# Two middle norms taken as one, table loads and weight splits moved to earlier places, in a kernel of two transformer blocks

## The chip, the cores and the metric

One core of a Trainium2 chip. The time is that of one execution on the device in microseconds (us); the kernel before takes 3049.42, the median of 3 runs. The engines are TensorE (PE: matmuls), VectorE (DVE), ScalarE (ACT), GpSimd (POOL) and SyncE (SP, which issues most of the DMA).

## The reference, cut to what matters

There are 16 meta tokens and 512 real ones, of width 1024. The first block is attention, the HGRN2 recurrence, a gated mix of both and a mixture of 32 experts, and ends with a norm. The second block begins with its own meta tokens and another norm, and is a feed-forward part (FFN 1), a mixer of Fourier, convolution and delta branches, and a second feed-forward part (FFN 2).

```python
def rms_norm(x, w):
    y = x * lax.rsqrt(jnp.mean(x * x, axis=-1, keepdims=True) + EPS)
    return y * w
...
    # end of first_block
    h = h + moe_out.reshape(B, L, D)
    return rms_norm(h, norm_final_w)[:, N_META:]
...
    # start of second_block
    h = jnp.concatenate([meta, x], axis=1)
    h = h + 0.5 * rmsnorm(swiglu(rmsnorm(h, n[0]), ffn1_wi[l], ffn1_wo[l]), n[1])
    h = h + rmsnorm(hybrid_mixer(rmsnorm(h, n[2]), ...), n[3])
    h = h + 0.5 * rmsnorm(swiglu(rmsnorm(h, n[4]), ffn2_wi[l], ffn2_wo[l]), n[5])
```

Each expert e takes its rows of tokens and computes (silu(a) * u) @ w_out[e], where a and u are the halves of x @ w_in[e].

## The kernel before

The hidden state `hT` stays in SBUF with the 1024 features on 8 x 128 partitions and the 528 tokens along the free dimension. Everything runs through in one program. Each engine has its own instruction order, which follows the order of the Python code, and semaphores tie the orders together.

**Split products.** A product in float32 is taken as three products of fp32r parts: each weight tile of 128x1024 is cast on ACT (`cast_act`, L424), and the rest, weight minus cast, is formed on DVE (`rest_dve`, L430). The input `uT` is cast on ACT (`high_act`, L459) into `fuh` or another `...uh`, and its rest formed on DVE (`low_dve`, L465). `Split` holds the weight tiles of a stage; SP loads them some tiles ahead into the slots of `ring`. Every stage begins by casting the first two or three tiles.

**Norm.** For each of 8 feature tiles ACT squares (`square_act`, L335), PE adds over the partitions by a product with a matrix of ones (`sum_pe`), ACT takes Ln (L374) and Exp with the factor -0.5 (L377), and DVE scales (`scale_dve`, L384). Ln and Exp stand in different tables of ACT. An activation of one element on `warm` (L371) loads the table of Ln ahead of it.

**Joins.** Between attention, `Hgrn`, `MixOut`, the experts and what follows, all engines but SP wait for the last signals of the stage in front (`join`, L269). At the start of `Hgrn` DVE also zeroes `Kl` and `sc` (L1088, L1089), and makes the rests of the three tiles of head 0. Attention goes in 32 steps of a head and a block of queries: PE scores, DVE `sm` (the row maximum, L717), ACT exp into `P` (L658), DVE reciprocal and scale, PE transpose, PE product.

**Route and Experts.** `Route` sends each token to two experts; `gates` is the weight of each row, `ov` the number of blocks beyond the 64 rows that an expert has (0 here). Weights come in chunks of 1 MB, 4 for w_in and 2 for w_out of each expert, issued on SP as slots come free. For expert e PE computes in(e) (4 chunks, from `exT`), then turns the product of e-1 (`turn_pe`, L1733) and computes out(e-1) (2 chunks, from `ehT`). Two experts' outputs are put into one tile `uT`, split into `uTr`, and put on their tokens by products with a matrix of zeros and ones, `eto` (`to_pe`): 8 for each pair of experts, 4 in each expert's turn, one behind each chunk of in(e). DVE adds each to `hT` (`add_dve`, L1806). `pool` gathers rows of tokens from DRAM.

**Overflow and BlockEnd.** After the last expert each engine reads `ov` (`values_load`, L1843) and branches around the code for further blocks (L1861), which ends in a barrier of all engines. `BlockEnd` takes the final norm of the first block in place on `hT` (with the weights `fin`), loads the second block's meta tokens, `m2T`, into the first 16 columns, and squares and sums again for the first norm of FFN 1, whose root and scaling stand in `Ffn`. `ConvFourier.act`, the first stage of the mixer, issues 7 DMA of Fourier tables from ACT's queue (L2343, L2344).

## Time and profile before

| | us |
|---|---|
| median of 3 runs (lowest, highest) | 3049.42 (3048.24, 3050.43) |
| the profiled execution: its time, its span | 3054.2, 3052.9 |
| PE busy in the span | 2751.3 (90%) |
| DVE, ACT, GpSimd busy | 1218.6, 933.0, 153.2 |
| mean granted clock of TensorE | 0.955 of full speed |

The span is the time in the records of one profiled execution. Busy shares are means over stages that have different limits. In the windows below the columns are the busy time of each engine, in brackets its number of instructions, then PEclk, the granted clock of TensorE as a share of 2.4 GHz (0.50 is the level of 1.2 GHz), the mean busy share of the 16 DMA engines, and what they moved.

### The profile page before, as it was taken

To read this page: it belongs to the slowest core of one execution; us is meant where nothing else is said; L and a number is where in the kernel's file an instruction comes from. 1 tells how busy PE (TensorE), PEld (TensorE's weight loads), DVE (VectorE), ACT (ScalarE), POOL (GpSimd) and SP (SyncE) were. 2 spreads that over 40 slices of the span, in tenths; PEclk is the share of its full clock that TensorE was granted. 3 is DMA by queue.
4 is the path that set the end of the run, shared out by engine and by line. 5 is a ranking of instruction groups with operands and counts; after the bars stand their busy time and mean duration, and the time that the engine had idled before them with its cause. 6 is when DMAs were issued, how large, how long until landed. Compare 5 with 4: busy or idle time off the path is not lost. (4 is left out here: it accounts for less than half of the span.)

```text
span 3052.9 us, 38074 instructions
## 1 busy us (share of the span) xinstructions
PE 2751.3 (90%) x15996; PEld 2092.7 (69%) x15996; DVE 1218.6 (40%) x2176; ACT 933.0 (31%) x1354; POOL 153.2 (5%) x210
## 2 busy tenths in 40 slices
PE   7989999898789988879999879898989898799997
PEld 6768888675333333359999878687868775578785
DVE  4346666534333333343333433243534334533334
ACT  4235555323111111142121341343434322422222
POOL 0000000000100000000000000121212110000000
PEclk9999999998899999989999989998989999899998
DMA  3012111234999999722222122111111122222221
GB/s 128 15 63 66 59 59 53 76 105 175 347 392 396 390 396 397 322 77 89 92 84 87 59 93 70 65 46 45 51 40 53 38 66 94 76 95 89 92 90 56
DMA packets 79177, 388.21 MB, mean 127 GB/s; under 512 B 9224, under 2 KB 9608, under 8 KB 53792
## 3 DMA queue, kind: packets, MB, share of 16 engines
q1 hardware_dynamic: 71856, 357.14, 32.5%
q0 software_dynamic: 5424, 23.35, 2.2%
q10 hardware_dynamic: 1728, 5.28, 0.5%
q8 instruction: 129, 2.11, 0.3%
q14 instruction: 40, 0.33, 0.0%
HBM read 375.10 MB, written 10.62 MB: 126 GB/s over the span
## 5 line engine op out<-in xcount | busy, mean ns | idle before, releaser
L197 PE MATMUL ps<-uTr,ringr 128*128 128x512 f32 (+1 forms) x1408 | 416.3, 342 | 0.0
L197 PE MATMUL ps<-muh,ringr 128*128 128x264 f32 (+1 forms) x1504 | 381.5, 346 | 25.2 <-DVE uTr L465 17.2
L197 PE MATMUL ps<-buh,ringr 128*128 128x512 f32 (+1 forms) x1312 | 352.7, 356 | 21.0 <-DVE ringr L430 15.5
L430 DVE TENSOR_TENSOR ringr<-ring,ringr 128x1024 fp32r<-128x1024 f32 (+1 forms) x215 | 257.6, 1210 | 255.2 <-ACT ringr L424 254.9
L197 PE MATMUL ps<-fuh,ringr 128*128 128x264 f32 (+1 forms) x1296 | 282.9, 324 | 19.2 <-DVE ful L465 19.2
L197 PEld LDWEIGHTS ps<-muh,ringr 128*128 128x128 f32 x1504 | 250.1, 196 | 53.1 <-issue 23.3
L424 ACT CAST ringr<-ring 128x1024 fp32r<-128x1024 f32 (+1 forms) x215 | 219.2, 1037 | 163.2 <-DMA ring<-in_w_fi 37.9
L197 PEld LDWEIGHTS ps<-uTr,ringr 128*128 128x128 f32 x1408 | 248.4, 195 | 24.4 <-issue 3.1
L197 PEld LDWEIGHTS ps<-buh,ringr 128*128 128x128 f32 x1312 | 222.4, 192 | 54.1 <-issue 26.1
L197 PEld LDWEIGHTS ps<-fuh,ringr 128*128 128x128 f32 x1296 | 203.3, 190 | 42.5 <-issue 18.6
L197 PE MATMUL ps<-rmore,exT 128*64 128x512 f32 x736 | 180.0, 612 | 7.7 <-DMA rmore<-in_w_ein 5.8
L197 PE MATMUL ps<-ful,ringr 128*128 128x264 f32 (+1 forms) x648 | 174.4, 324 | 0.0
L1806 DVE TENSOR_TENSOR hT<-hT,ps 128x512 f32<-128x512 f32 x128 | 87.7, 687 | 207.1 <-PE ps L197 207.0
L2122 DVE TENSOR_TENSOR fsg<-ps,fsg 128x528 f32<-128x528 f32 (+1 forms) x44 | 30.8, 699 | 301.7 <-PE ps L197 301.7
L197 PE MATMUL ps<-fhh,ringr 128*128 128x264 f32 (+1 forms) x576 | 126.3, 326 | 4.4 <-DVE fhl L465 4.4
L197 PEld LDWEIGHTS ps<-eto,uTr 128*128 128x128 f32 x256 | 39.1, 192 | 126.2 <-issue 122.0
L1767 ACT COPY exT<-ps 128x512 f32<-128x512 f32 x32 | 18.7, 585 | 339.1 <-PE ps L201 339.1
L197 PEld LDWEIGHTS ps<-rmore,exT 128*64 128x64 f32 x736 | 50.4, 138 | 99.2 <-issue 84.9
L197 PE MATMUL ps<-eto,uTr 128*128 128x512 f32 x256 | 93.7, 452 | 25.3 <-DVE uTr L1796 24.8
L197 PEld LDWEIGHTS ps<-ful,ringr 128*128 128x128 f32 x648 | 109.2, 190 | 9.6
L459 ACT CAST fhh<-fsg 128x528 fp32r<-128x528 f32 (+1 forms) x44 | 27.6, 627 | 254.0 <-DVE fsg L2122 254.0
L197 PE MATMUL ps<-rmore,ehT 128*64 128x512 f32 x384 | 87.7, 597 | 17.5 <-DVE ehT L1780 16.4
(436 smaller groups left out, 4473.7 us busy)
## 6 DMA issues: line engine op xcount, KB each, us to landing
rmore<-in_w_ein SPq DMA_DIRECT2D x92, 1024.0 KB, 27.6
rmore<-in_w_eout SPq DMA_DIRECT2D x48, 1024.0 KB, 27.7
ring<-in_w_ein SPq DMA_DIRECT2D x36, 1024.0 KB, 28.8
ring<-in_w_fi SPq DMA_DIRECT2D x54, 512.0 KB, 3.7
fmore<-in_w_fi SPq DMA_DIRECT2D x34, 512.0 KB, 3.8
ring<-in_w_hg SPq DMA_DIRECT2D x32, 512.0 KB, 3.8
ring<-in_w_eout SPq DMA_DIRECT2D x16, 1024.0 KB, 28.9
ring<-in_w_out SPq DMA_DIRECT2D x32, 512.0 KB, 3.8
```

What stands on the lines that cost most here:

```text
L197: return self.P.matmul(out, lhsT, rhs, start=start, stop=stop, skip_group_check=True)
L424: self.k.A.copy(self.halves(i)[0], self.part(i)).then_inc(self.cast.next(), 1)
L430: self.k.V.tensor_tensor(low, self.part(i), high.bitcast(F32), SUB).then_inc(self.rest.next(), 1)
L459: (self.k.A.copy(h, src) if scale == 1.0 else self.k.A.mul(h, src, scale)).then_inc(self.high.next(), 1)
L1767: A.copy(self.xT[:, e % 2].rearrange("p a c -> p (a c)"), k.ps[:, self.bank("x", e), :]).then_inc(self.x_out.next(), 1)
L1806: k.V.tensor_tensor(h, h, k.ps[:, self.bank("to", n), :], ADD).then_inc(self.added.next(), 1)
L2122: V.tensor_tensor(self.row(s), self.acc(self.bank[i + 1]), self.row(s), MUL).then_inc(self.prod.next(), 1)
```

## The change

1. `Norm.table_act`: the load of Ln's table goes ahead of the first square, instead of behind the last. That holds for every norm.
2. At three joins the first tiles' casts and rests are made in the stage in front: of head 0's tiles in attention's steps 25 to 30 (the loads too), of `MixOut`'s first two in `Hgrn`'s last steps, and in `Ffn` and `ConvFourier` all but the first tile are cast and their rests made between the scalings of the norm. `Kl` and `sc` are zeroed on GpSimd, behind the issue of the spill of `hT`.
3. `m2T` is loaded at the start of `Route.pool`; its 16 columns' norm is taken in small pieces (`meta_dve`, `meta_pe`, `meta_act`) at the first expert.
4. All five engines wait for `ov` and read it ahead of the experts. The barrier of all engines behind the branch goes.
5. In the experts the four products with `eto` of an expert's turn stand behind chunks 1 to 3 and behind `turn_pe`, instead of behind chunks 0 to 3. DVE's adds follow: three at the start of a turn and the fourth behind the product with the gates.
6. `BlockEnd` becomes one norm of the 512 real columns. Its 8 squares are summed twice: on PE with the weights fin² + EPS in the columns' place of the ones (bank 6), and on DVE into `acc`, which one product with ones then sums over the partitions (bank 7). Two Ln and one Exp give the scale of the first norm of block 2 at once; `uT` is `hT` times that times `fin` times the gain. The scaling of `hT` itself comes later: an Exp behind `Ffn`'s casts (`late_act`) and 8 DVE instructions in the second group of FFN 1 (`late_dve`). Before, there were 8 scalings of `hT`, a second set of 8 squares, 16 sums of 264 columns and a second Ln.
7. The 7 DMA of Fourier tables go from ACT's queue to GpSimd's.

```diff
+    def table_act(self):
+        self.k.A.activation(self.k.warm, self.k.eps, ACT.Ln)
     def square_act(self, x, m, *values):
         k = self.k
+        if m == 0:
+            self.table_act()
...
-        k.A.activation(k.warm, k.eps, ACT.Ln)
...
+                if n in (25, 27, 29):
+                    self.ahead.cast_act((n - 25) // 2)
...
+                if n in (26, 28, 30):
+                    self.ahead.rest_dve((n - 26) // 2)
...
+    def pool(self):
+        G = self.k.G
+        G.memset(self.Kl, 0.0).then_inc(self.zero.next(), 1)
+        G.memset(self.sc, 0.0).then_inc(self.zero.next(), 1)
...
+                if h == 9 and n in (4, 5):
+                    self.ahead.cast_act(n - 4)
...
-        V.memset(self.Kl, 0.0).then_inc(self.zero.next(), 1)
-        V.memset(self.sc, 0.0).then_inc(self.zero.next(), 1)
...
+                    self.ahead.rest_dve(n - 4)
...
-        W.cast_act(0)
-        W.cast_act(1)
...
-        W.rest_dve(0)
-        W.rest_dve(1)
...
+        G.dma_start(k.hT[:, :, 0:NM], k.a["m2T"]).then_inc(k.ld_m2.landing(), 16)
...
+        self.nxt.meta_dve()
...
+                if e == 0:
+                    self.nxt.meta_pe()
             else:
-                for n in self.steps(e):
+                for n in self.steps(e)[0:3]:
                     self.to_pe(n)
             if e + 1 < NE:
                 self.rows_pe(e + 1)
             if e:
                 self.turn_pe(e - 1)
+                for n in self.steps(e)[3:]:
+                    self.to_pe(n)
...
-            if beside:
-                self.to_pe(beside[c])
+            if beside and c:
+                self.to_pe(beside[c - 1])
...
+            for n in self.steps(e)[0:3]:
...
+            for n in self.steps(e)[3:]:
+                self.add_dve(n)
+            if e == NE:
+                self.nxt.weights_dve(self.comb.at(4 * NE - 8))
...
-        nc.all_engine_barrier()
...
+    def meta_dve(self):
+        k, V, x = self.k, self.k.V, self.k.hT[:, :, 0:NM]
+        y = k.sq[:, 0, 0:8 * NM].rearrange("p (a c) -> p a c", a=8)
+        V.wait_ge(*k.ld_m2.at(16))
+        V.tensor_tensor(y, x, x, MUL).then_inc(self.small.next(), 1)
...
+        self.table_act()
         for m in range(8):
-            self.norm.square_act(k.hT, m)
-        self.norm.root_act()
+            if m >= 2:
+                k.A.wait_ge(*self.sumsq.at(m - 1))
+                k.A.wait_ge(*self.gathered.at(m - 1))
+            k.A.activation(k.sq[:, m % 2, 0:S], k.hT[:, m, NM:L], ACT.Square).then_inc(self.square.next(), 1)
...
+        k.take(6, 7)
+        P.wait_ge(*self.weighted.at(1))
         for m in range(8):
-            self.nxt.square_act(k.hT, m, self.norm.scaled.at(m + 1), k.ld_m2.at(16))
-    def pe(self):
+            P.wait_ge(*self.square.at(m + 1))
+            k.mm(k.ps[:, 6, :], self.weights[:, 128 * m:128 * m + 128], k.sq[:, m % 2, 0:S], m == 0, m == 7).then_inc(
+                self.sumsq.next(), 1)
+        P.wait_ge(*self.gathered.at(8))
+        k.mm(k.ps[:, 7, :], k.ones, self.acc, True, True).then_inc(self.mean.next(), 1)
...
+    def root_act(self):
+        k, rb, r = self.k, self.k.rb[:, NM:L], self.k.sq[:, 0, 0:S]
+        k.A.wait_ge(*self.sumsq.at(8))
+        k.A.activation(rb, k.ps[:, 6, :], ACT.Ln, bias=k.eps2[:, 0:1], scale=1.0 / D).then_inc(self.log.next(), 1)
+        k.A.wait_ge(*self.mean.at(1))
+        k.A.activation(r, k.ps[:, 7, :], ACT.Ln, bias=k.eps[:, 0:1], scale=1.0 / D).then_inc(self.rlog.next(), 1)
+        k.A.wait_ge(*self.log.at(1))
+        k.A.activation(rb, rb, ACT.Exp, scale=-0.5).then_inc(self.root.next(), 1)
...
+            V.wait_ge(*self.root.at(1))
+        V.scalar_tensor_tensor(out=out[:, m, c], in0=x[:, m, c], scalar=k.fin[:, 1, m:m + 1], in1=k.rb[:, c], op0=MUL,
+                               op1=MUL).then_inc(self.scaled.next(), 1)
...
             exp.sp()
+            exp.first_pool()
+            for eng in (k.P, k.V, k.A, k.G, k.SP):
+                eng.wait_ge(*route.blocks.last())
+            count = k.nc.values_load(route.ov[0:1, 0:1], min_val=0, max_val=NOV - 1)
...
-        for i in range(3):
-            W.cast_act(i)
+        W.cast_act(0)
         self.norm.root_act()
         for m in range(8):
             self.norm.high_act(self.pu, m)
+            if m in (3, 6):
+                W.cast_act(m // 3)
...
+            if m in (5, 7):
+                W.rest_dve(m // 2 - 1)
...
+                if g == 1:
+                    self.norm.late_dve(j)
...
-        for n in range(NC2):
-            A.dma_start(self.dft[:, n].rearrange("p a c -> p (a c)"), k.a["dft"][n]).then_inc(self.there[n].landing(), 16)
-        A.dma_start(self.dfs, k.a["dfs"]).then_inc(self.there_s.landing(), 16)
...
+        G.dma_start(self.dfs, k.a["dfs"]).then_inc(self.there_s.landing(), 16)
+        for n in range(NC2):
+            G.dma_start(self.dft[:, n].rearrange("p a c -> p (a c)"), k.a["dft"][n]).then_inc(self.there[n].landing(), 16)
```

Line numbers in the rows of the changed kernel below are its own: L430 of before is L443, L717 is L736, L335 is L342, L1733 is L1768, L197 is L198 and L1806 is L1847.

PE in the turn of expert 31 and behind it, before (`exT` is the input of in(e), `ehT` of out(e), `eto,uTr` the products with the matrix of zeros and ones, `con,eact` is `turn_pe`; a row "x2" is one `to_pe`):

```order
L197 MATMUL ps<-rmore,exT 64x512 x4
L197 MATMUL ps<-eto,uTr 128x512 x2
L1733 MATMUL ps<-con,eact 128x64 x4
L197 MATMUL ps<-rmore,ehT 64x512 x8
L197 MATMUL ps<-eto,uTr 128x512 x8
L1733 MATMUL ps<-con,eact 128x64 x4
L197 MATMUL ps<-rmore,ehT 64x512 x8
L197 MATMUL ps<-eto,uTr 128x512 x16
L1843 TENSOR_LOAD ov
```

The same place in the changed kernel:

```order
L198 MATMUL ps<-rmore,exT 64x512 x4
L198 MATMUL ps<-eto,uTr 128x512 x2
L1768 MATMUL ps<-con,eact 128x64 x4
L198 MATMUL ps<-eto,uTr 128x512 x2
L198 MATMUL ps<-rmore,ehT 64x512 x8
L198 MATMUL ps<-eto,uTr 128x512 x6
L1768 MATMUL ps<-con,eact 128x64 x4
L198 MATMUL ps<-eto,uTr 128x512 x2
L198 MATMUL ps<-rmore,ehT 64x512 x8
L198 MATMUL ps<-eto,uTr 128x512 x16
L211 COMPARE_AND_BRANCH
```

One product with `eto` now stands between `turn_pe` and the product that waits for DVE's copy of what was turned, and the read of `ov` is gone from here.

ACT from the end of the experts to FFN 1's first casts, before:

```order
L1861 UNCONDITIONAL_BRANCH
L335 ACTIVATE sq<-hT 128x512 x8
L371 ACT_TABLE_LOAD
L371 ACTIVATE warm<-eps 128x1
L374 ACTIVATE rb<-ps,eps 128x512
L377 ACT_TABLE_LOAD
L377 ACTIVATE rb<-rb 128x512
L335 ACTIVATE sq<-hT 128x528 x8
L424 CAST ringr<-ring 128x1024 x3
L371 ACT_TABLE_LOAD
L371 ACTIVATE warm<-eps 128x1
L374 ACTIVATE rb<-ps,eps 128x528
```

In the changed kernel (`fuh` is the high part of `uT`):

```order
L333 ACT_TABLE_LOAD
L333 ACTIVATE warm<-eps 128x1
L2040 ACTIVATE sq<-hT 128x512 x8
L437 CAST ringr<-ring 128x1024
L2078 ACTIVATE rb<-ps,eps 128x512
L2080 ACTIVATE sq<-ps,eps 128x512
L2082 ACT_TABLE_LOAD
L2082 ACTIVATE rb<-rb 128x512
L472 CAST fuh<-uT 128x528 x4
L437 CAST ringr<-ring 128x1024
L472 CAST fuh<-uT 128x528 x3
L437 CAST ringr<-ring 128x1024
```

Eight squares, three table loads and two casts of weights no longer stand ahead of the first cast of `uT`; one further Ln does.

DVE at the end of attention and the start of `Hgrn`, before (`sm` is the maximum of a row of scores, `P` the exp of them, `PT` its transpose, `lbv` and the like are small constants of `Hgrn`):

```order
L722 TENSOR_SCALAR P<-P,sm 128x528
L728 COPY PT<-ps 128x384
L728 COPY PT<-ps 128x512
L1075 TENSOR_TENSOR lbv<-vec 128x8
...
L1087 TENSOR_SCALAR hnh<-vec 128x1
L1088 MEMSET hKl 128x3584
L1089 MEMSET hsc 128x1024
L430 TENSOR_TENSOR ringr<-ring,ringr 128x1024 x3
L1110 TENSOR_SCALAR hfs<-hfs,omv,lbv 128x528
```

In the changed kernel, from the copy ahead of step 30 (steps 26 and 28 have such a row as well):

```order
L747 COPY PT<-ps 128x128
L443 TENSOR_TENSOR ringr<-ring,ringr 128x1024
L736 TENSOR_REDUCE sm<-ps 128x1
L739 RECIPROCAL sm<-sm 128x1
L741 TENSOR_SCALAR P<-P,sm 128x400
L747 COPY PT<-ps 128x256
...
L1118 TENSOR_SCALAR hnh<-vec 128x1
L1141 TENSOR_SCALAR hfs<-hfs,omv,lbv 128x528
L1146 TENSOR_SCALAR hk<-hfs 128x528
```

A rest of a weight tile now stands ahead of a row maximum in attention, and the two memsets and three rests are gone from the start of `Hgrn`.

## Rows read from the trace of the kernel before

**Rows 1.** The page, busy time, share of the span and instructions of each engine:

```profile
PE 2751.3 (90%) x15996; PEld 2092.7 (69%) x15996; DVE 1218.6 (40%) x2176; ACT 933.0 (31%) x1354; POOL 153.2 (5%) x210
```

**Rows 2.** Timeline, first norm: start, us, engine, line, operation, [idle before <-releaser]

```profile
18.48 1.28 ACT L371 ACT_TABLE_LOAD   x1
```

**Rows 3.** DVE's waits, attention's last steps (172 to 197 us): total, times, longest

```profile
DVE sm L717 <- PE ps L197: 2.9, 4, 0.8
```

**Rows 4.** Timeline, start of `Hgrn`

```profile
196.36 0.58 ACT L668 COPY oaT<-ps 128x512 f32<-128x512 f32 x1 [2.28 <-PE ps L197]
...
199.50 3.04 DVE L1088 MEMSET hKl<- 128x3584 f32 x1 [0.69 <-issue]
...
203.53 3.43 DVE L430 TENSOR_TENSOR ringr<-ring,ringr 128x1024 fp32r<-128x1024 f32 x3
...
204.95 0.78 PE L197 MATMUL ps<-buh,ringr 128*128 128x264 f32 x2 [8.62 <-DVE ringr L430]
```

**Rows 5.** Window behind that start (columns as told above)

```profile
205.00:211.00 6.00, 6.00 (x27) 6.00 (x28) 1.96 (x2) 0.00 (x0) 0.00 (x0) 0.50 0.00 0
```

**Rows 6.** Timeline, from `Hgrn` to `MixOut`

```profile
587.87 2.94 ACT L424 CAST ringr<-ring 128x1024 fp32r<-128x1024 f32 x3 [1.55 <-DVE oh L1204]
...
590.52 0.77 PE L197 MATMUL ps<-buh,ringr 128*128 128x512 f32 x1 [6.87 <-DVE ringr L430]
```

**Rows 7.** Timeline, end of `Route` and first expert

```profile
781.69 1.11 PE L201 MATMUL ps<-con,xg 64*128 64x64 f32 x8
...
783.24 0.58 ACT L1767 COPY exT<-ps 128x512 f32<-128x512 f32 x1 [23.09 <-PE ps L201]
...
783.92 4.78 PE L197 MATMUL ps<-rmore,exT 128*64 128x512 f32 x12 [1.12 <-DVE rgates L1608]
...
784.77 0.13 DVE L1615 CAST ov<-rnb 1x1 int32<-1x1 f32 x1
787.63 0.33 SPq L250 DMA_DIRECT2D rmore<-in_w_eout  x1
```

**Rows 8.** A window in the experts

```profile
800.00:1030.00 230.00, 209.28 (x1006) 76.95 (x1004) 77.21 (x113) 33.59 (x52) 13.91 (x15) 1.00 1.01 390
```

**Rows 9.** PE's waits in the experts (790 to 1300 us): total, times, longest

```profile
PE ps L197 <- DVE uTr L1796: 24.8, 16, 3.2
PE ps L197 <- DVE ehT L1780: 22.1, 30, 0.9
```

**Rows 10.** Timeline, end of the experts

```profile
1247.79 8.65 SPq L250 DMA_DIRECT2D rmore<-in_w_eout  x4
...
1289.16 3.65 PE L197 MATMUL ps<-rmore,ehT 128*64 128x512 f32 x16 [0.93 <-DVE ehT L1780]
...
1295.98 6.59 PE L197 MATMUL ps<-eto,uTr 128*128 128x512 f32 x16 [3.17 <-DVE uTr L1796]
```

**Rows 11.** The page's DMA issues: operation, count, KB each, median us from issue to landing

```profile
rmore<-in_w_eout SPq DMA_DIRECT2D x48, 1024.0 KB, 27.7
```

**Rows 12.** Timeline, `BlockEnd` to FFN 1

```profile
1307.81 0.63 ACT L335 ACTIVATE sq<-hT 128x512 f32<-128x512 f32 x1 [13.19 <-PEq L1861]
...
1318.68 0.67 ACT L374 ACTIVATE rb<-ps,eps 128x512 f32<-128x512 f32 x1
...
1337.36 0.64 ACT L377 ACTIVATE rb<-rb 128x528 f32<-128x528 f32 x1
...
1340.42 0.78 PE L197 MATMUL ps<-fuh,ringr 128*128 128x264 f32 x2 [8.10 <-DVE ful L465]
```

**Rows 13.** Timeline, FFN 1 to the mixer

```profile
1758.74 2.85 ACTq L2343 DMA_DIRECT2D dft<-in_dft  x6
...
1770.53 0.78 PE L197 MATMUL ps<-muh,ringr 128*128 128x264 f32 x2 [11.88 <-DVE uTr L465]
```

**Rows 14.** Timeline, the mixer to FFN 2

```profile
2642.72 2.94 ACT L424 CAST ringr<-ring 128x1024 fp32r<-128x1024 f32 x3 [1.26 <-PE ps L197]
```

**Rows 15.** GpSimd's groups by form: busy, mean ns, idle before

```profile
L3194 POOL TENSOR_TENSOR nDT<-nDT,nKK 88x528 f32<-88x528 f32 x8 | 12.5, 1561 | 17.1 <-DVE nMT L3107 17.1
```

More of the change, by code:

```diff
@@ L1335, in block1 @@
             k.G.dma_start(k.spill1, k.hT).then_inc(k.spilled.landing(), 16)
+            rec.pool()
             rec.sp()
+            for w, n in (("w_oh", 8), ("w_o", 4)):
+                for m in range(n):
+                    for x in range(2):
+                        W2.load(k.a[w][m, :, 1024 * x:1024 * x + 1024])
             rec.pe()
@@ L1340, in block1 @@
             k.join(*rec.sigs, k.spilled)
-            k.sig.close(loads)
+            k.sig.close(loads + W2.sigs)
         norm = Norm(k, NM, True)
-        mix = MixOut(k, st, oh, branch.gt, norm)
-        mix.sp()
+        mix = MixOut(k, st, oh, branch.gt, norm, W2)
         mix.pe()
@@ L1937, in dve, with __init__, constants_dve, meta_pe @@
         ins.then_inc(self.summed.next(), 1)
-class BlockEnd:
-    def __init__(self, k, nxt):
-        self.k, self.norm, self.nxt = k, Norm(k, NM), nxt
-        k.ld_m2 = k.sig.pdma("m2")
-    def pool(self):
-        k = self.k
-        k.G.dma_start(k.hT[:, :, 0:NM], k.a["m2T"]).then_inc(k.ld_m2.landing(), 16)
+class BlockEnd(Norm):
+    def __init__(self, k):
+        Norm.__init__(self, k, 0)
+        sig = k.sig
+        flat = k.uT.rearrange("p a c -> p (a c)")
+        self.weights, self.acc = flat[:, 0:1024], flat[:, 2048:2560]
+        k.ld_m2 = sig.pdma("m2")
+        self.small, self.weighted, self.gathered, self.scale_h = (sig.dve(n) for n in (
+            "fsmall", "fweights", "fgathered", "fscaled"))
+        self.msum, self.mlog, self.mroot = sig.pe("msum"), sig.act("mlog"), sig.act("mroot")
+        self.mean, self.rlog, self.rroot = sig.pe("fmean"), sig.act("rlog"), sig.act("rroot")
+        self.sigs += [self.small, self.weighted, self.gathered, self.scale_h, self.msum, self.mlog, self.mroot, self.mean,
+                      self.rlog, self.rroot, k.ld_m2]
+    def constants_dve(self):
+        k, V, g, fin = self.k, self.k.V, self.k.vec["fin"], self.k.fin
+        V.memset(k.eps2, EPS * EPS).then_inc(self.small.next(), 1)
+        V.tensor_tensor(fin[:, 0, :], g, g, MUL).then_inc(self.small.next(), 1)
+        V.tensor_tensor(fin[:, 1, :], g, k.vec["g"][:, 0:8], MUL).then_inc(self.small.next(), 1)
+        V.wait_ge(*self.small.at(2))
+        V.tensor_scalar(fin[:, 0, :], fin[:, 0, :], EPS, None, ADD).then_inc(self.small.next(), 1)
+    def meta_dve(self):
[3 more added lines that the diff above has]
+        V.tensor_tensor(y, x, x, MUL).then_inc(self.small.next(), 1)
+    def meta_pe(self):
+        k = self.k
+        k.take(7)
+        k.P.wait_ge(*self.small.at(5))
+        for m in range(8):
+            ins = k.mm(k.ps[:, 7, 0:NM], k.ones, k.sq[:, 0, NM * m:NM * m + NM], m == 0, m == 7)
+        ins.then_inc(self.msum.next(), 1)
+        k.give((7,), self.mlog.at(1))
+    def meta_act(self):
+        k, A, rb = self.k, self.k.A, self.k.rb[:, 0:NM]
+        A.wait_ge(*self.msum.at(1))
+        A.activation(rb, k.ps[:, 7, 0:NM], ACT.Ln, bias=k.eps[:, 0:1], scale=1.0 / D).then_inc(self.mlog.next(), 1)
+        A.wait_ge(*self.mlog.at(1))
+        A.activation(rb, rb, ACT.Exp, scale=-0.5).then_inc(self.mroot.next(), 1)
@@ L1960, in pe, with weights_dve, dve @@
+    def weights_dve(self, free):
+        k, V = self.k, self.k.V
+        V.wait_ge(*free)
         for m in range(8):
-            self.norm.sum_pe(m)
+            ins = V.tensor_scalar(self.weights[:, 128 * m:128 * m + 128], k.ones, k.fin[:, 0, m:m + 1], None, MUL)
+        ins.then_inc(self.weighted.next(), 1)
+    def dve(self):
+        k, V = self.k, self.k.V
         for m in range(8):
-            self.nxt.sum_pe(m)
-    def dve(self):
-        k = self.k
-        for m in range(8):
-            self.norm.scale_dve(k.hT, [k.vec["fin"][:, i:i + 1] for i in range(8)], k.hT, m)
+            V.wait_ge(*self.square.at(m + 1))
+            if m:
+                V.wait_ge(*self.gathered.at(m))
+                V.tensor_tensor(self.acc, self.acc, k.sq[:, m % 2, 0:S], ADD).then_inc(self.gathered.next(), 1)
+            else:
+                V.tensor_copy(self.acc, k.sq[:, 0, 0:S]).then_inc(self.gathered.next(), 1)
@@ L1971, in experts, with late_act, late_dve @@
+    def late_act(self):
+        k, r = self.k, self.k.sq[:, 0, 0:S]
+        k.A.wait_ge(*self.rlog.at(1))
+        k.A.activation(r, r, ACT.Exp, scale=-0.5).then_inc(self.rroot.next(), 1)
+    def late_dve(self, m):
+        k, h = self.k, self.k.hT[:, m, NM:L]
+        k.V.wait_ge(*self.rroot.at(1))
+        k.V.scalar_tensor_tensor(out=h, in0=h, scalar=k.vec["fin"][:, m:m + 1], in1=k.sq[:, 0, 0:S], op0=MUL,
+                                 op1=MUL).then_inc(self.scale_h.next(), 1)
 def experts(k, norm, free, kept):
+    end = BlockEnd(k)
@@ L1974, in experts @@
     with ExitStack() as st:
-        route = Route(k, st, norm)
+        route = Route(k, st, norm, end)
+        end.constants_dve()
         route.pe()
@@ L1987, in experts @@
             exp.pool()
-            k.join(*exp.sigs, *exp.got, route.blocks)
+            k.join(*exp.sigs, *exp.got)
             k.SP.wait_ge(*exp.added.last())
-            k.SP.wait_ge(*route.blocks.last())
         with ExitStack() as st2:
-            Overflow(k, st2, route).run()
-    nxt = Norm(k, 0)
-    end = BlockEnd(k, nxt)
+            Overflow(k, st2, route).run(count)
     end.pe()
```

118 lines of the change are left out of this document (72 added, 46 removed).

## The prediction

> **What bounds the kernel now.** I read the page first: PE is busy for 2751.3 us of 3052.9 [rows 1]. So the time that is left to win lies in the stretches where PE waits. The list of waits by line then says what PE waits for. The timeline of each stretch says which chain of instructions ends last. Last, windows by stage tell whether PE or the DMA sets the pace. Two kinds of stretch appear. At the joins of stages PE stands still for 8.62 us before `Hgrn` [rows 4], 6.87 before `MixOut` [rows 6], 8.10 before FFN 1 behind two norms in a row [rows 12] and 11.88 before the mixer [rows 13]. There a chain on ACT and DVE bounds the time. In the experts PE waits in many small pieces for DVE [rows 9], but the 16 DMA engines are busy without a gap, share 1.01 [rows 8]. The sum goes from the start of the program to its end.
>
> **First norm.** Ln's table load, 1.28 us [rows 2], goes ahead of the squares, where ACT waits for its input. ACT has casts to make until right before it, so all of it is on the path: gain 1.3.
>
> **Attention to Hgrn.** PE can start when the last copy of attention ends, at 196.36 + 0.58 = 196.9, and starts at 204.95 [rows 4]. The three rests and two memsets are all that is between, so the gain is up to 8.0; I take 7.9. Right behind the start six us run at a granted clock of 0.50, with 27 matmuls [rows 5]; at full clock they would take 3.0. The engine had stood still for 8.6 us before. With no such stop I expect most of it back, 2.6, between 0 and 3.0. Against it, attention is lengthened. Three rests of 1.22 (3.43 for three that overlap a little, rows 4) come ahead of the row maxima of steps 26, 28 and 30. In eight steps DVE waits four times for the scores, 2.9 in all, 0.8 at the longest [rows 3]; the three rests meet about three of these waits, 2.3 us. So 3.7 - 2.3 = 1.4 are lost, and 3.7 at most. Sum: 7.9 + 2.6 - 1.4 = 9.1.
>
> The memsets go behind a DMA issue on GpSimd. The nearest row there is a tensor-tensor of 528 elements in 1.56 us [rows 15], which for 3584 and 1024 elements would make 10.6 and 3.0. DVE takes 3.04 and 0.91 [rows 4], the lower bound. Even 13.6 from 198 ends at 212, and `Kl` is first written some 30 us behind the start of `Hgrn`. Cost 0.
>
> The Trainium skill (SBUF — State Buffer, Who interferes with whom) speaks against this: a `tensor_scalar` of DVE can take a pair of ports that it shares with GpSimd, and whichever engine issues first holds them for the whole instruction. By that rule the two `TENSOR_SCALAR` of DVE that make `hfs` and `hk` would stand until the memset is done. No row of before has such a pair at once; by the rule the sum would be up to 2 us worse, and without it it takes 0.
>
> **Hgrn to MixOut.** PE starts at 590.52, the first cast at 587.87 [rows 6]. With both made earlier 2.65 go. One rest of 1.2 now stands ahead of the last copy that the chain needs, and the cast ahead of it waits for a gate; half is hidden at a guess, bounds 0 and 1.2. Gain 1.9.
>
> **Route.** This one loses. The first expert's product starts at 783.92, while DVE is at work on `ov` until 784.77 + 0.13 = 784.90 [rows 7]. Now every engine waits for `ov` and reads it before its first expert instruction. The small square of `meta_dve` adds 0.3, the read 0.5 (no row shows it; bounds 0 and the 4.5 that read, branch and barrier take together below), then come the eight transposes of the first rows, 1.1, the copy of 0.58 [rows 7] and 0.4 of handing over: 787.7. DMA goes on only when PE frees a slot, at 787.63 today [rows 7], so all of it shifts too. Loss 3.8, bounds 3 and 7.
>
> **Experts.** PE goes from 783.92 [rows 7] to the start of out(31) at 1289.16 [rows 10] in 32 turns of 15.8 us. The waits for `uTr`, 24.8, and `ehT`, 22.1 [rows 9], are 1.5 of each; work is 14.3. Moving one product with `eto` behind `turn_pe` (0.8 = 6.59 / 8, rows 10) covers the waits of 0.7 for `ehT`, and starting them one chunk later, 1.9 or more, covers most of those of 1.5 for `uTr`. Is that 47 us? The 14 slots are filled before the experts, and the other 178 of 192 chunks land between 787.63 and the last landing. The last of four issues, 8.65 in all, begins at 1254.3 [rows 10], and 27.7 later [rows 11] is 1282.0. That makes 2.78 per chunk and 16.7 per expert, at a DMA share of 1.01. So DMA sets the body's pace now, and PE only lives off the lead of 14 chunks. A faster PE will use up that lead and wait for chunks: body 0.
>
> At the end it counts. Out(31) ends at 1289.16 + 3.65 = 1292.8 [rows 10], 10.8 behind the last landing. PE that keeps up is through with out(30) at 1278.8: its last chunk lands two chunks of 2.5 (1 MB at 420 GB/s, an estimate for the end of the stream) before 1282.0, and half of 3.65 follows. Then come three products with `eto` 2.5, a turn 0.5, one more 0.8, and out(31) 3.65; with 0.5 for handing over it ends at 1286.8. Gain 6.0, bounds 3 and 7.
>
> **Overflow, BlockEnd, FFN 1.** The experts' last add ends 0.7 behind the products, 1295.98 + 6.59 + 0.7 = 1303.3 = T [rows 10]. PE starts FFN 1 at 1340.42 = T + 37.1 [rows 12]. After the change: branch, table load and its activation 1.6 (the load now stands behind the branch, where nothing hides it); squares and sums 1318.68 - 1307.81 = 10.9 as today; one product with ones 1.0; Ln 0.67, table 1.28; and from the start of Exp to PE's start 1340.42 - 1337.36 = 3.1 [rows 12, 2]. That is 18.5, a gain of 18.6. The barrier, the 8 scalings, the second squares, sums and Ln are gone with it. DVE's sums of squares, 0.7 each, run beside PE's of 1 us. Against it, two rests of 1.22 are now inside the chain of scalings and rests which feeds PE until its end: 2.4. Gain 16.2. At full clock the sums would be 2.9 shorter.
>
> **FFN 1 to the mixer.** From 1758.74 the Fourier issues hold ACT for 3.4, the second cast 1.0, and table and activation 1.4, all ahead of Ln [rows 13, 14]; one rest inside the chain costs 1.2. Gain 4.6. The tables on GpSimd's queue are first wanted some 30 us later: cost 0.
>
> **Mixer to FFN 2.** Two casts of the three in 2.94 [rows 14] and table and activation: 3.4, less two rests: 0.9.
>
> **Nothing.** `meta_pe`, `meta_act` with three table loads and `weights_dve` stand in the experts, where DVE and ACT are idle for two thirds and more [rows 8]; `late_act` and the 8 `late_dve` in FFN 1, where PE bounds. Without that cover they would be some 2, 5, 1 and 6 us.
>
> **Sum.** 1.3 + 9.1 + 1.9 - 3.8 + 0 + 6.0 + 16.2 + 4.6 + 0.9 = 36.2. The profiled execution took 3054.2, 4.8 over the median of the runs. 3054.2 - 36.2 = 3018.0, and as a median 3013.
>
> **Rivals.** *Less is won (0.17).* The clock stays at half speed behind each join (-2.6), the rests cost attention all of 3.7 (-2.3), the experts start 7 us late (-3.2), the tail gives 3 (-3), the rest before `MixOut` is all on the path (-0.6): 12 less, 3025. For it speaks that the window behind the join is slow today; against it, that these are several small things.
>
> *More is won (0.14).* The sums run at full clock (2.9) and the rests at the joins hide (2.4, 1.2, 2.4): 9 more, 3004. The 6 us stop before the squares is gone, which speaks for it; that DVE has no gap in these chains, against it.
>
> *The memset is in the way (0.08).* GpSimd's memset lasts to 212 by the bound above. `hfs` comes on DVE some 9 us behind PE's start, at about 206; if DVE has to stand until 212, the rest of the next tile behind it is done at 214, about when PE comes to it: 0 to 2 us, 3015. The skill's sentence on the shared ports is for it, GpSimd's unknown pace (3 to 10.6 us) leaves it open.
>
> *The body is PE's (0.03).* If DMA can go faster when it is asked sooner, the 47 us less the 6 already counted come on top: 2972. The share of 1.01 speaks against it.
>
> *Slower (0.04).* PE's waits turn into waits for chunks. If the granted clock, 1.00 today [rows 8], falls to half for a share s of the experts, PE's work is 14.3 x (1 + s). It passes DMA's 16.7 at s = 0.17, and eats the 36 us at s = 0.25, since each 0.01 is 4.6 us. At a third of the time it is 3054. PE's busy share doesn't fall against today's, which speaks against it.
>
> **How the numbers follow.** The forecast itself has 0.54, 3013 with 3008 to 3020 as its own range. To leave out no more than two in ten I reach over the case of more and that of less, with some us beyond for the bound of 7 at the experts' start and of 0 for the clock: 3002 to 3029. A change under 0.2% (6 us) can't be told from none here. Faster 0.94, the same 0.02, slower 0.04.
>
> **What would show it.** In the changed profile: PE's start of `Hgrn` near 198 and `MixOut` without a stop; the first expert's product about 3 us behind the last cast of `ov`; waits for `uTr` and `ehT` replaced by waits for `rmore`; out(31) within 5 us of the last landing; 18 to 21 us from the last add to FFN 1. Wrong would be: a granted clock of 0.5 in the experts, a DMA share clearly below 1, or attention longer by over 4 us.

## The result and the profile after

The changed kernel takes 3014.97 us, the median of 4 runs (3012.9 to 3016.04), beside 3049.93 for the kernel before on the same chip (3048.24 to 3053.38). The ratio is 0.9883, with an interval of 0.9866 to 0.99. The forecast was 3013 with a range of 3002 to 3029. Of the kernel before there are two profiled executions in all, of 3052.9 and 3046.9 us span, and of the changed one three, of 3014.7, 3007.4 and 3016.0. The first of each is read here, the others where it matters.

The page of the changed kernel: PE is as busy as before and the span shorter, so the time came out of PE's stops.

```profile
span 3014.7 us, 38051 instructions
PE 2750.9 (91%) x15982; PEld 2090.1 (69%) x15982; DVE 1224.6 (41%) x2197; ACT 927.6 (31%) x1347; POOL 161.5 (5%) x219
```

**Start of `Hgrn`.** Timeline of the changed kernel, the columns as in [rows 4]:

```profile
194.44 0.59 ACT L685 COPY oaT<-ps 128x512 f32<-128x512 f32 x1 [2.28 <-PE ps L198]
195.13 0.48 PE L198 MATMUL ps<-buh,ringr 128*128 128x264 f32 x2 [0.72 <-PE ps L198]
196.15 3.11 POOL L910 MEMSET hKl<- 128x3584 f32 x1
196.66 3.53 DVE L1117 TENSOR_SCALAR omv<-lbv 128x8 f32<-128x8 f32 x1
199.18 0.97 POOL L911 MEMSET hsc<- 128x1024 f32 x1
201.92 0.56 DVE L1141 TENSOR_SCALAR hfs<-hfs,omv,lbv 128x528 f32<-128x528 f32 x1 [1.73 <-ACT hfs L1043]
```

PE's stop of 8.62 [rows 4] is 0.72. GpSimd zeroes `hKl` in 3.11, hardly slower than DVE's 3.04, and nothing like the bound of 10.6. The row to look at is DVE's: a `TENSOR_SCALAR` of 8 elements takes 3.53 us, and ends at 200.19, when GpSimd's second memset ends (199.18 + 0.97). The next large DVE instruction, `hfs`, begins at 201.92, behind its own input.

The window behind the start:

```profile
197.00:203.00 6.00, 6.00 (x44) 5.63 (x43) 4.23 (x5) 2.00 (x4) 3.16 (x2) 1.00 0.85 339
```

The granted clock is 1.00 where it was 0.50 [rows 5], 44 matmuls in 6 us for 27.

**Hgrn to `MixOut`.** Timeline:

```profile
566.11 1.98 ACT L437 CAST ringr<-ring 128x1024 fp32r<-128x1024 f32 x2
567.17 1.23 DVE L443 TENSOR_TENSOR ringr<-ring,ringr 128x1024 fp32r<-128x1024 f32 x1 [1.91 <-ACT ringr L437]
568.32 0.68 DVE L1228 COPY ho<-ps 128x512 f32<-128x512 f32 x1
575.17 0.80 PE L198 MATMUL ps<-buh,ringr 128*128 128x512 f32 x1 [4.27 <-DVE oh L1235]
```

PE starts 0.05 behind `oh` instead of 2.68 [rows 6]. The copy of `ho` stands behind the rest and begins 1.4 behind its product instead of 0.04. From its start to the end of `oh` it is 0.8 shorter, so the rest costs 0.6.

**Route and the first expert.** Timeline:

```profile
765.68 0.14 DVE L1644 CAST ov<-rnb 1x1 int32<-1x1 f32 x1
766.64 1.08 PE L202 MATMUL ps<-con,xg 64*128 64x64 f32 x8 [4.27 <-DVE ov L1644]
768.45 8.76 PE L198 MATMUL ps<-rmore,exT 128*64 128x512 f32 x32 [0.72 <-issue]
772.09 2.04 SPq L251 DMA_DIRECT2D rmore<-in_w_eout  x2
```

The transposes of the first rows now wait 4.27 for `ov`. The product starts 2.6 behind the end of the cast of `ov`; before it began 1.0 ahead of that [rows 7]. SP goes on 3.6 behind the product, as before.

**The experts.** PE's waits from 770 to 1285 us, total, times, longest:

```profile
PE ps L198 <- DMA rmore<-in_w_ein: 20.2, 16, 2.3
PE ps L198 <- DMA ring<-in_w_ein: 10.6, 8, 2.3
```

And a window, with the columns of [rows 8]:

```profile
1000.00:1200.00 200.00, 179.50 (x820) 63.86 (x818) 65.86 (x97) 27.55 (x43) 10.85 (x12) 0.97 1.01 396
```

PE no longer waits for `uTr` and `ehT` [rows 9] but for chunks of the weights, 31 us in all for 47 before. The DMA share is 1.01, as before [rows 8]. The granted clock is 0.97 in this window: short patches at the lower clock appear. Up to the start of out(31) there are six, of 3.4 us each, where the experts had one before.

**End of the experts, FFN 1.** Timeline:

```profile
1230.76 8.67 SPq L251 DMA_DIRECT2D rmore<-in_w_eout  x4
1267.00 3.65 PE L198 MATMUL ps<-rmore,ehT 128*64 128x512 f32 x16 [0.26 <-DVE ehT L1817]
1280.09 1.28 DVE L1847 TENSOR_TENSOR hT<-hT,ps 128x512 f32<-128x512 f32 x2 [0.23 <-PE ps L198]
1281.57 1.28 ACT L333 ACT_TABLE_LOAD   x1 [9.10 <-DVE hT L1847]
1282.97 1.13 ACT L2040 ACTIVATE sq<-hT 128x512 f32<-128x512 f32 x2
1292.74 1.02 PE L198 MATMUL ps<-uT,o 128*128 128x512 f32 x2
1298.77 0.78 PE L198 MATMUL ps<-fuh,ringr 128*128 128x264 f32 x2 [5.01 <-DVE ful L478]
1306.21 0.52 PE L198 MATMUL ps<-fuh,ringr 128*128 128x264 f32 x2 [1.06 <-DVE ful L478]
```

The last of four issues of weights begins at 1237.3, and out(31) starts 29.7 later, where it was 34.9 [rows 10]. Against the landing of the last chunk it starts 0.6 behind and ends 4.3 behind; before, these were 7.2 and 10.8. From the first product to that landing it is 497.9 us, and it was 498.1. PE starts FFN 1 17.4 behind the last add (1280.09 + 1.28). In the last row it waits for a low part that stands behind a rest.

**Mixer and FFN 2.** Timeline:

```profile
1719.99 3.18 POOL L2490 DMA_DIRECT2D dft<-in_dft  x6
1724.89 0.78 PE L198 MATMUL ps<-muh,ringr 128*128 128x264 f32 x2 [6.03 <-DVE uTr L478]
2612.24 0.77 PE L198 MATMUL ps<-fuh,ringr 128*128 128x512 f32 x1 [5.96 <-DVE ful L478]
```

The stop before the mixer is 6.03 instead of 11.88 [rows 13]. That before FFN 2 is 5.96 and was 9.36:

```profile
2652.00 0.77 PE L197 MATMUL ps<-fuh,ringr 128*128 128x512 f32 x1 [9.36 <-DVE ful L465]
```

### The profile page after: what moved, and what is told of

It is laid out like the page before. It is cut to its first block and busy times, and to the rows that moved or that the text cites. A ratio compares the mean times of both kernels' runs of the same rounds, so it can differ in the third digit from the quotient of the medians.

```text
span 3014.7 us, 38051 instructions
## 1 busy us (share of the span) xinstructions
PE 2750.9 (91%) x15982; PEld 2090.1 (69%) x15982; DVE 1224.6 (41%) x2197; ACT 927.6 (31%) x1347; POOL 161.5 (5%) x219
## 5 line engine op out<-in xcount | busy, mean ns | idle before, releaser
L198 PE MATMUL ps<-uTr,ringr 128*128 128x512 f32 (+1 forms) x1408 | 415.8, 341 | 0.0
L198 PE MATMUL ps<-muh,ringr 128*128 128x264 f32 (+1 forms) x1504 | 384.1, 348 | 20.0 <-DVE uTr L478 11.9
L443 DVE TENSOR_TENSOR ringr<-ring,ringr 128x1024 fp32r<-128x1024 f32 (+1 forms) x215 | 258.5, 1211 | 252.7 <-ACT ringr L437 252.1
L198 PE MATMUL ps<-buh,ringr 128*128 128x512 f32 (+1 forms) x1312 | 350.3, 353 | 9.8 <-DVE oh L1235 4.3
L198 PE MATMUL ps<-fuh,ringr 128*128 128x264 f32 (+1 forms) x1296 | 283.3, 324 | 16.0 <-DVE ful L478 15.9
L198 PEld LDWEIGHTS ps<-muh,ringr 128*128 128x128 f32 x1504 | 253.1, 198 | 47.8 <-issue 17.5
L198 PEld LDWEIGHTS ps<-uTr,ringr 128*128 128x128 f32 x1408 | 247.5, 195 | 23.6 <-issue 3.1
L198 PEld LDWEIGHTS ps<-buh,ringr 128*128 128x128 f32 x1312 | 220.8, 190 | 42.8 <-issue 8.9
L198 PEld LDWEIGHTS ps<-fuh,ringr 128*128 128x128 f32 x1296 | 204.1, 191 | 39.6 <-issue 12.6
L198 PE MATMUL ps<-rmore,exT 128*64 128x512 f32 x736 | 181.5, 622 | 21.7 <-DMA rmore<-in_w_ein 20.2
L1847 DVE TENSOR_TENSOR hT<-hT,ps 128x512 f32<-128x512 f32 x128 | 87.7, 688 | 219.2 <-PE ps L198 218.2
L198 PE MATMUL ps<-ful,ringr 128*128 128x264 f32 (+1 forms) x648 | 174.8, 324 | 0.0
L198 PEld LDWEIGHTS ps<-rmore,exT 128*64 128x64 f32 x736 | 52.8, 140 | 121.7 <-issue 85.3
L198 PE MATMUL ps<-fhh,ringr 128*128 128x264 f32 (+1 forms) x576 | 124.9, 323 | 4.4 <-DVE fhl L478 4.4
L198 PEld LDWEIGHTS ps<-ful,ringr 128*128 128x128 f32 x648 | 108.8, 190 | 9.1
L198 PEld LDWEIGHTS ps<-fhh,ringr 128*128 128x128 f32 x576 | 90.0, 189 | 13.6 <-DVE fhl L478 5.0
L198 PEld LDWEIGHTS ps<-eto,uTr 128*128 128x128 f32 x256 | 39.9, 195 | 85.8 <-issue 79.8
L198 PE MATMUL ps<-eto,uTr 128*128 128x512 f32 x256 | 95.7, 459 | 4.0 <-DVE uTr L1837 3.2
```

The source lines that it names most:

```text
L198: return self.P.matmul(out, lhsT, rhs, start=start, stop=stop, skip_group_check=True)
L443: self.k.V.tensor_tensor(low, self.part(i), high.bitcast(F32), SUB).then_inc(self.rest.next(), 1)
L1847: k.V.tensor_tensor(h, h, k.ps[:, self.bank("to", n), :], ADD).then_inc(self.added.next(), 1)
```

## The experiments

All but the controls and the last undo or alter one thing in the changed kernel. A whole execution of one and the same kernel varies by several us from one to the next. So most verdicts rest on a stretch between two instructions in the profile, and the time of the whole is given beside it.

### Controls

The first profiles held a surprise: from PE's start of the mixer to its start of FFN 2 it took 881.5 us before and 887.4 after, though the stop at the end of this stretch is 3.4 shorter, and the rest at its start costs only 1.1 (see the rests below). The stretch to compare lies between: from DVE's last low part at the mixer's start to ACT's first square for FFN 2. PE's matmuls and DVE's instructions there are the same and in the same order in both kernels; the loads of Ln's table stand elsewhere in the norms, so that ACT has one more in the stretch, and the 7 DMA of Fourier tables come from another queue.

> The kernel before, profiled once more. Between the first squares of the mixer and those of FFN 2 the changed kernel took some 8 us longer than the kernel before, with the same instructions there. Theory: this is where patches of the lower granted clock fall in one execution, so this second profile of the same kernel has that stretch differ from the first by up to 4 us or more, with the low patches in other places. Rival: the change itself slows the mixer; then this stretch agrees with the first profile within 1 us.

> The changed kernel, profiled once more. Theory: the mixer's stretch comes out shorter or longer than in its first profile by several us, and the sum of low-clock time explains it at half its length. Rival: it is again 8 us longer than in the kernel before, whatever the clock does.

The kernel before took 3048.25, the changed one 3008.71. The stretch between, in the first profiles of both kernels and in that of the kernel with the tables back on ACT's queue (an experiment below):

```profile
1778.95:2631.60 852.65, 767.42 (x4911) 629.68 (x4909) 316.86 (x520) 290.80 (x419) 116.34 (x163) 0.94 0.18 59
1734.45:2595.46 861.01, 773.83 (x4911) 633.15 (x4909) 316.88 (x520) 292.15 (x422) 116.92 (x163) 0.93 0.19 58
1738.60:2591.96 853.36, 768.34 (x4911) 630.87 (x4909) 316.83 (x519) 292.12 (x421) 116.22 (x163) 0.94 0.18 59
```

The second profile of the kernel before gives 852.8, within 0.1 of its first. So the first expectation failed, and what came is what its rival had named. The changed kernel gives 861.0, 854.4 and 857.3 in its three profiles. The eight other kernels below that have the tables on GpSimd's queue lie between 854.1 and 859.0 (in two of them a rest of 1.1 moves into the stretch and is counted in it). All eleven are longer than the kernel before, by 4.2 in the mean without that rest. The mixer is slower in the changed kernel, and a part of what the joins win is lost there.

The second expectation holds in kind: the changed kernel's two profiles differ by 6.6. In the stretch the first has 120.3 us at the lower clock and the second 110.1; the 10.2 are worth 5.1 at half speed, most of the 6.6. The kernel before has 103 in both. So the loss looks like the clock's: 7 to 17 us more at the lower level. What in the change brings the patches isn't shown. The one kernel with the tables on ACT's queue has 102.8 us at the lower clock and 853.4 in all, nearly as before. That is a single profile, and it makes the queue of the tables the first suspect, no more.

### The order of products in the experts

```diff
-            if beside and c:
-                self.to_pe(beside[c - 1])
+            if beside:
+                self.to_pe(beside[c])
```

The fourth product behind `turn_pe` and the split of DVE's adds go too.

> The changed kernel with the four products with ones of an expert's turn back behind chunks 0 to 3, and the adds back at the head of the turn. Theory (DMA sets the body's pace): the last landing moves by under 1 us against the first product, PE waits for ehT and uTr again, and out(31) ends 5 to 7 us later; the kernel takes 6 us more than the changed one, ratio to before about 0.990 to 0.991. Rival (PE sets the pace): the body is some 40 us longer, ratio about 1.0.

Waits of this kernel, 770 to 1300 us:

```profile
PE ps L198 <- DVE uTr L1833: 23.5, 15, 3.2
PE ps L198 <- DVE ehT L1815: 22.4, 30, 0.9
PE ps L198 <- DMA rmore<-in_w_ein: 3.8, 3, 1.5
```

The waits of before are back, 46 us, and the time isn't. From the first product to the last add it takes 517.9 us; the changed kernel takes 512.9, 512.6 and 514.3 in its three profiles, and before it was 519.4 and 518.1. So 46 us of waits are worth 3.5 to 5.3. They count at the end: the last chunk lands 497.9 us behind the first product, as in the changed kernel's first profile, and out(31) starts 5.6 behind that landing instead of 0.6. DMA sets the pace of the body, and the rival that PE does is out by 35 us. The whole took 3017.17 (0.9889, interval 0.9872 to 0.9906), which fits and tells nothing by itself.

The order also moves the clock. Between the first product and out(31) this kernel has no patch at the lower clock behind the first 5 us, and the kernel before none or one. The changed kernel has six, six and four, and the eight others with its order three to six. DMA's pace hides them there.

### Head 0's splits

```diff
-                if n in (25, 27, 29):
-                    self.ahead.cast_act((n - 25) // 2)
...
-                if n in (26, 28, 30):
-                    self.ahead.rest_dve((n - 26) // 2)
```

`Hgrn` then makes them at its start. The memsets stay on GpSimd.

> The changed kernel with the casts and rests of head 0's first three tiles back at the start of Hgrn; the memsets stay on GpSimd. Theory 1 (the clock follows PE's stop, and GpSimd's memset holds DVE up): DVE's small tensor_scalar stand until the memset of 3.1 us ends, the first rest follows, PE starts 5.5 to 6.5 us behind the last copy of attention in place of 0.7, and the window behind it runs at 0.5 for some 6 us, which costs 2.5 more; attention is 0.7 shorter. In all 7 to 8 us more than the changed kernel. Rival A (no port is held): PE starts 3.5 behind the copy. Rival B (the clock's patch has nothing to do with the stop): the window stays at 1.0, 5 us more in all.

Timeline of its start of `Hgrn`, and the window behind:

```profile
192.66 3.10 POOL L906 MEMSET hKl<- 128x3584 f32 x1
193.17 3.51 DVE L1113 TENSOR_SCALAR omv<-lbv 128x8 f32<-128x8 f32 x1
193.46 3.22 DVE L443 TENSOR_TENSOR ringr<-ring,ringr 128x1024 fp32r<-128x1024 f32 x1
195.68 0.97 POOL L907 MEMSET hsc<- 128x1024 f32 x1
196.98 0.78 PE L198 MATMUL ps<-buh,ringr 128*128 128x264 f32 x2 [6.06 <-DVE ringr L443]
```

```profile
197.00:203.00 6.00, 6.00 (x28) 6.00 (x29) 0.00 (x0) 0.00 (x0) 0.00 (x0) 0.51 0.22 93
```

Theory 1 holds at the join. DVE's `TENSOR_SCALAR` ends at 196.68, with GpSimd's second memset (196.65). The first rest behind it ends at 196.68 too, 3.22 where one takes 1.22: PE starts 2.0 later than by its own work. PE starts 5.4 behind the copy of attention's last output (0.1 in the changed kernel), and behind the stop the clock is 0.51, where the changed kernel has 1.00. From the copy's end to `hfs` it is 14.8 us against 6.9: 7.9 lost, of which 2.6 are the clock's. Attention is 0.5 shorter: from the 25th row maximum to the last copy it takes 24.0, as in both profiles of the kernel before, and 24.5 in the changed kernel.

The whole disagrees: 3012.91 (0.9873, interval 0.9855 to 0.9891), no slower than the changed kernel. An expected 7 us should show beside an interval of some 5, and doesn't. Its profile doesn't win the time back in one place; against the second profile of the changed kernel it ends 8.3 later, against the first 1.0 later. That the stop costs over 7 us there is shown; that the kernel as a whole is 7 us slower is not.

### The memsets

```diff
-        G.memset(self.Kl, 0.0).then_inc(self.zero.next(), 1)
+        V.memset(self.Kl, 0.0).then_inc(self.zero.next(), 1)
```

The same for `sc`, at DVE's place of before, with the splits of head 0 in attention.

> The changed kernel with the two memsets of Hgrn on DVE, the splits of head 0 still in attention. Theory: DVE's small tensor_scalar are back at 0.17 us, its memsets end about 4 us later, hfs waits for PE's product anyway, and its distance from PE's start of Hgrn stays 6.8 us; the move to GpSimd of the memsets by itself buys and costs nothing. Rival 1 (the port pair cost up to 2 us): hfs comes earlier here. Rival 2: hfs comes later here, since the memsets on DVE end behind the product.

DVE's timeline of this kernel:

```profile
196.91 0.17 DVE L1115 TENSOR_SCALAR omv<-lbv 128x8 f32<-128x8 f32 x1
197.83 3.04 DVE L1117 MEMSET hKl<- 128x3584 f32 x1 [0.69 <-DVE hnh L1116]
202.17 0.56 DVE L1141 TENSOR_SCALAR hfs<-hfs,omv,lbv 128x528 f32<-128x528 f32 x1 [0.22 <-ACT hfs L1041]
```

The small instruction is back at 0.17, so its 3.5 was GpSimd's memset. `hfs` comes 6.8 behind PE's start in both kernels. The theory holds: with the splits in attention, moving the memsets is worth nothing. 3012.80 in one run.

### The barrier

```diff
+        nc.all_engine_barrier()
```

behind the branch, where it was.

> The changed kernel with the barrier of all engines behind the branch put back. Theory: it holds every engine for about 3.5 to 4 us behind the last add (the 4.5 that read, branch and barrier took before, less 0.5 for the read), so FFN 1 starts 21 to 22 us behind the last add in place of 17.5, and the sums may run at the lower clock, some us more. Rival: ACT's table load, 1.5 us, goes on beside it and the squares lose only 2 us.

```profile
1282.68 1.28 ACT L333 ACT_TABLE_LOAD   x1 [12.96 <-PEq L1903]
1300.55 0.78 PE L198 MATMUL ps<-fuh,ringr 128*128 128x264 f32 x2 [5.00 <-DVE ful L478]
```

FFN 1 starts 21.9 behind the last add, which ends at 1278.65, instead of 17.4: 4.5. The table load doesn't go on beside the barrier: it starts 4.0 behind the last add instead of 0.2, so the barrier holds it for 3.8, and GpSimd's `DRAIN` takes 3.58 of that. The other 0.7 are the 16 sums on PE, 9.8 for 9.2: in the whole stretch 10.7 us are at the lower clock, for 4.7. 3012.64 in one run.

### The Fourier tables

> The changed kernel with the 7 DMA issues of Fourier tables back on ACT's queue. Theory: ACT casts and takes Ln 3.3 to 3.4 us later, and PE stands still 9.4 us before the mixer in place of 6.0. Rival: a part of the issues hides behind PE's sums, and the stop grows by 2 us or less.

The edit puts the two loops of issues back ahead of `W.cast_act(0)`.

```profile
1719.53 3.02 ACTq L2489 DMA_DIRECT2D dft<-in_dft  x6
1729.03 0.78 PE L198 MATMUL ps<-muh,ringr 128*128 128x264 f32 x2 [9.59 <-DVE uTr L478]
```

A stop of 9.59 for 6.03: the issues were wholly on the path at this join, 3.6. 3009.62 in one run, which is no longer than the changed kernel: the mixer behind the join takes 853.4, as told under the controls, and from FFN 2's start to the end it is 399.3 for 402.5, with 20.4 us at the lower clock for 27.0. So whether the move of the tables wins anything in the whole stays open; one profile can't tell.

### Rests behind the last low part

```diff
-            if m in (5, 7):
-                W.rest_dve(m // 2 - 1)
         self.pu.low_dve(k.uT[:, 7, r0:L], k.uh[:, 7, r0:L], self.ul[:, 7, r0:L], 7)
+        W.rest_dve(1)
+        W.rest_dve(2)
```

and in the mixer's first stage the same with its one rest.

> The changed kernel with the rests of the second and third weight tile of both FFNs, and of the second of the mixer, behind the last low part of the input instead of between the scalings. Theory: PE walks through the first tile behind DVE's low parts, so a rest in that chain costs its whole 1.22; behind it, it hides under PE's last products of the first tile and the second tile's 6 us. Gain about 2 at each FFN and 1 at the mixer, 5 us against the changed kernel. Rival: PE waits for the rest of the second tile instead, and nothing or under 1 us is won at each.

DVE's timeline at FFN 1:

```profile
1305.32 0.71 DVE L478 TENSOR_TENSOR ful<-uT,fuh 128x528 fp32r<-128x528 f32 x1 [0.28 <-ACT fuh L472]
1305.95 2.35 DVE L443 TENSOR_TENSOR ringr<-ring,ringr 128x1024 fp32r<-128x1024 f32 x2
```

From PE's start to the end of the last low part it is 8.5, 8.4 and 8.4 us at FFN 1, the mixer and FFN 2, for 10.4, 9.6 and 10.3: 1.9, 1.1 and 1.9 won, 4.9 in all. PE doesn't wait for these rests. The theory holds. 3005.92 (0.9855, interval 0.9839 to 0.9872), 9 below the changed kernel's median; what is beyond 4.9 isn't explained, and whole runs vary by as much.

### The first expert ahead of the read

```diff
+            exp.head_pe()
+            exp.rows_act(0)
             for eng in (k.P, k.V, k.A, k.G, k.SP):
                 eng.wait_ge(*route.blocks.last())
```

`head_pe` holds the first rows' transposes and in(0).

> The changed kernel with the first expert's rows, their copy on ACT and its product in(0) issued on PE and ACT ahead of the wait for ov and its read. Theory: the product starts when the gates' matmuls end, as before the change, 3 to 4 us earlier against the gates' copy on DVE, all of the stream of weights shifts with it and the kernel takes 3.5 us less than the changed one. Rival: the wait moves with the read to behind in(0) and holds PE up there by as much, while DMA, which has 4 free slots by then, still gains; then 3.5 as well at the last landing, but PE waits behind in(0).

```profile
762.67 1.08 PE L202 MATMUL ps<-con,xg 64*128 64x64 f32 x8 [1.06 <-DMA xg<-vrow,idx]
764.56 4.70 PE L198 MATMUL ps<-rmore,exT 128*64 128x512 f32 x14 [0.80 <-issue]
768.00 0.33 SPq L251 DMA_DIRECT2D rmore<-in_w_eout  x1
```

The product comes 2.8 behind the copy of the gates, for 4.6 in the changed kernel and 0.8 before. So 1.8 are won, not 3.8: the transposes now wait for the gather of their rows instead of for `ov`, and start 5.5 behind its issue at 757.17 (4.4 before the change). SP follows the product by 3.4, and PE doesn't wait behind in(0), against the rival. 3008.77 (0.9866, interval 0.985 to 0.9883).

### Ln's table behind the second square

```diff
-        self.table_act()
         for m in range(8):
+            if m == 2:
+                self.table_act()
```

> The changed kernel with the load of Ln's table in BlockEnd behind the second of its 8 squares instead of ahead of the first. Theory: ACT waits 1.6 us for PE's first sum there, so the load of 1.28 and its activation hide, the first square starts 1.5 earlier and PE starts FFN 1 15.8 us behind the last add in place of 17.3. Rival: the third square comes late by what doesn't fit, and PE's sums wait for it: 0.5 or less is won.

```profile
1281.25 1.28 ACT L333 ACT_TABLE_LOAD   x1
1295.90 0.56 PE L198 MATMUL ps<-fuh,ringr 128*128 128x264 f32 x1 [5.00 <-DVE ful L478]
```

FFN 1 starts 16.0 behind the last add (it ends at 1279.87), for 17.3: 1.3 of 1.5 are won. 3006.27 in one run.

### All three together

> The changed kernel with the three edits together: rests behind the last low part, first expert ahead of the read of ov, Ln's table behind the second square. From the stretches measured: 1.9 + 1.1 + 1.9 for the rests, 1.8 for the first expert, 1.5 for the table by theory, 8.2 in all, so 3004 to 3007 on this chip, ratio to before 0.985 to 0.986. Rival: the clock's patches eat some of it, and it is not to be told from the changed kernel.

> The changed kernel itself, timed beside the kernel with the three edits. Expected 3011 to 3016; the other is 5 to 10 us below it.

3006.79 (0.9857, interval 0.984 to 0.9875), beside 3014.98 for the changed kernel on the same chip (0.9882, interval 0.9863 to 0.9901). The difference is the expected 8.2. The intervals overlap, so by the timing alone it is likely and not certain. The stretches are shorter in the profile: product behind the gates 1.6, FFN 1 behind the last add 15.0, low parts 8.5, 8.4 and 8.4.

## Why the prediction came out right, by its steps

| step | forecast | in the profiles |
|---|---|---|
| first norm | 1.3 | 1.5 for the table; 1.1 more in the squares, which vary as much from profile to profile of one kernel |
| attention | -1.4 | -0.5 |
| stop before `Hgrn` | 7.9 | 7.9 |
| clock behind it | 2.6 | 2.7; 2.0 against the second profile of before |
| Hgrn to `MixOut` | 1.9 | 2.6 less 0.6 |
| Route | -3.8 | -3.8 |
| experts, first product to last add | 6.0 | 3.8 to 6.8; 3.5 to 5.3 with the order undone |
| last add to last low part of FFN 1 | 16.2 | 19.7 less 2.0 |
| mixer's start | 4.6 | 5.8 less 1.1 |
| mixer, last low part to first square of FFN 2 | 0, no term | -8.3, -1.7, -4.6 in three profiles |
| FFN 2's start | 0.9 | 3.4 less 2.1 |

Without the mixer's row the right column comes to near 39, from 36 to 42 over the pairs of profiles. The mixer takes back 4.9 in the mean. That leaves 34; the medians moved by 35.0 and the profiles by 38.2 and 39.5. So the terms of the joins and of the experts are sized well by their mechanisms, and together they are some 3 too small. That the forecast of 3013 is 2 us from the measured 3014.97 is in part luck: the 3 and the mixer's 4.9, which no step foresaw, have opposite signs.

**Steps that held.** Body 0 and tail 6 was the step with the most at stake, 41 us between it and the rival. It rested on the DMA share and on the landing of the last chunk, and undoing the order showed it: the last landing stayed and out(31) moved. The forecast had out(31) end 4.8 behind the last landing, and it is 4.3. That Route loses was right to 0.1, and its cause is the wait for `ov`, though taking that away gave back only half: the gather's landing is next in line, which I hadn't named. The Trainium skill (SBUF — State Buffer, Who interferes with whom) says that a `tensor_scalar` of DVE can contend with GpSimd for a shared pair of ports, and that the later of the two then stands for the whole instruction of the other. The trace agrees, with 3.5 us for 8 elements, and 0.17 with the memset on DVE; it adds that DVE stood until the second of two memsets in a row was done. It hit the small `TENSOR_SCALAR` that make `omv` and `hnh`, and not those of `hfs` and `hk` that the prediction named. I gave the collision 0 to 2 us. It is 0 as the change stands, and 2.0 where a rest that PE waits for stands behind, as in the kernel with head 0's splits back.

**Steps that were off.** The mixer had no term, and is longer by 1.7 to 8.3. The prediction priced the tables on GpSimd's queue at nothing, for the reason that they are first wanted late; what their move does to the granted clock behind it was not asked, and stays open. The bound of 10.6 for GpSimd's memset: a tensor-tensor with two inputs, 1.56 for 528 elements, says nothing of a memset, which ran at DVE's pace. The BlockEnd term was 1.5 too small. 1.1 of it lies between the last add and PE's start, and the rests cost 2.0 instead of 2.4. With that, 17.4 us from the last add to FFN 1 lies just under the 18 to 21 that the prediction gave as its sign. The rests cost attention 0.5 instead of 1.4; which further gap they use was not looked into.

**Rivals.** Slower, by TensorE at the lower clock in the experts: such patches did appear, six of 3.4 us in the first profile where before there was one, 4% of the stretch against the quarter from which it would have decided. For a third of the time the prediction wrote 3054; by its own rule, 4.6 us for each 0.01 beyond 0.17, it is 3089. Of the case of less only the tail came near its bound, with 3.8 in one pair of profiles for a bound of 3. More was won at BlockEnd by 1.5. That a stage without a change gets slower stood in no rival.

## What to carry to other kernels

Waits of an engine that total 46 us can be worth 5: ask first whether a saturated queue sets the pace, and then count only what happens behind its last landing. A cast or rest moved off a join should go behind the chain that feeds PE, not between its links; the same work there costs its full length. When two engines wait for a small result before they go on, look for what else lands just behind it before you price the wait. And where a control comes out as the rival said, follow the rival: here the kernel before repeated its mixer to 0.1 us, and the changed kernel never reached it.
